# Forgetting attention beside RWKV: the scores of the next row block are issued ahead of the turn of the present block's weights

## The chip, the cores and the metric

One Trainium2 chip, one core of it. The program is one launch. Its time is the device time in microseconds (us). A core has five engines that each run their own stream of instructions: TensorE (PE in the profile, its weight loads PEld), VectorE (DVE), ScalarE (ACT), GpSimd (POOL) and SyncE (SP, which issues most DMAs). They meet only through semaphores.

## The reference, cut to what matters

The reference is three layers in float32 on 1024 tokens of width 1024: a Hyena and differential attention layer, a hybrid of stick-breaking attention and two gated recurrences, and a layer with an RWKV recurrence beside forgetting attention. The change lies in the third layer's mixing. Of each of its 8 heads of 64 columns the forgetting attention computes

```
s[t, j] = q[t] . k[j] + c[t] - c[j]      for j <= t   (c: running sum of the log forget gates)
w[t, :] = softmax(s[t, :])
o[t]    = sum_j w[t, j] v[j]
```

The kernel puts c into two additional rows of q and k, so that one product over 66 rows gives s. The RWKV recurrence of 8 heads runs over 16 chunks of 64 tokens and shares nothing with the attention but the engines.

## The kernel before, in words

`rwkv_and_fox` (L3329) is one stage, named mix. It does RWKV and the forgetting attention together. Its work is cut into jobs, and `mix_jobs` (L3316) writes one list of 712 jobs: 416 of RWKV, 296 of attention. The first 14 are attention; from there on each RWKV job is followed by no or one attention job, so that both run out together. **TensorE, ScalarE and VectorE each walk through this same list in its order** (L3593, L3642, L3746) and issue what the job needs of them. An engine that waits for a semaphore holds all that stands behind it in its own stream. SP has its own order of loads (L3429 to L3449).

The attention of one head h goes over 8 row blocks i of 128 tokens. Block i has (i + 1) * 128 columns. `fox_jobs` (L3302) gives the order of its jobs:

- scores: TensorE multiplies q and k into the PSUM tile S (L3573 to L3575, the last one adds the causal mask); there is one S, so it waits until exp has read the block before (`exp_done`, L3569). VectorE takes the row maximum and negates it (L3734, L3735). ScalarE computes exp(S - max) into `Pr[i % 2]`, a double buffer in SBUF, with the row sum (L3632).
- weigh: VectorE takes the reciprocal of the sum and scales the block by it in place (L3738, L3739).
- turn: TensorE transposes up to four 128 x 128 tiles of the scaled block into the PSUM tile TP (L3582), ScalarE copies TP to SBUF as PT (L3640). Blocks 4 to 7 need two turns, (i, 0) for the first four tiles and (i, 1) for the rest. There is one TP: a turn waits until the copy of the turn before it is done (`turn_kept`, L3580).
- out: TensorE multiplies V with PT into the PSUM tile O (L3590); it waits for the copy of the block's last turn (L3585). VectorE copies O into Y (L3744).
- values: the transposes of V of two heads, ahead of every second head (L3559, copied in L3623); they also use TP.

An RWKV job is one product of 4 pairs of heads (8 matmul instructions in float32, L3458; the jobs sa and s have 16, y has 24) or 4 transposes (L3464: q4, an, vn, bhn, khn) into one of four PSUM banks, and then a copy by ScalarE (L3611) or a masked product or sum by VectorE (L3663 to L3722). A bank is used again four RWKV jobs later.

In the list, between the jobs of head 2, block 6 and the next stand these jobs (the number is the RWKV chunk):

```
weigh(2,6)  p4,5  h,4  turn(2,6,0)  ht,4  scores(2,7)  q4,4  h,5  turn(2,6,1)  ht,5  out(2,6)  q4,5  h2,4  weigh(2,7)
```

Of the kernel before, what the change touches and what calls it, by code (L numbers as in the profile page):

```python
# [3301 lines left out]
def fox_jobs(h):  # L3302

    jobs = [("values", h // 2, b) for b in range(2)] if h % 2 == 0 else []
    jobs.append(("scores", h, 0))
    for i in range(8):
        jobs += [("weigh", h, i), ("turn", h, i, 0)]
        if i < 7:
            jobs.append(("scores", h, i + 1))
        if i >= 4:  # L3310
            jobs.append(("turn", h, i, 1))
        jobs.append(("out", h, i))
    return jobs


def mix_jobs():  # L3316

    a, b = [job for g in range(8) for job in rwkv_jobs(g)], [job for h in range(8) for job in fox_jobs(h)]
    FIRST = 14
    jobs, taken = b[:FIRST], FIRST  # L3320
    for n, job in enumerate(a):
        jobs.append(job)
        until = FIRST + (n + 1) * (len(b) - FIRST) // len(a)
        jobs += b[taken:until]
        taken = until
    return jobs
# [723 lines left out]
```

How the kernel before makes its waits and increments, by code:

```python
    def step(self, ins):  # L59
        self.n += 1
        ins.then_inc(self.sem, 1)
        self.eng.wait_ge(self.sem, self.base + self.n)
# [21 lines left out]
            @block.sync  # L84
            def _(sp):
                for dst, src in pairs:
                    sp.dma_start(dst, src).then_inc(loaded, 16)
                sp.wait_ge(loaded, 16 * len(pairs))
# [53 lines left out]
    def fetch(self, sp, n, kp, tiles):  # L142
        if n == 0 and self.ahead is not None:
            return
        if n >= self.slots:
            sp.wait_ge(self.phases_done, 7 * (n - self.slots + 1))
        for i, src in enumerate(tiles):
            sp.dma_start(self.W[n % self.slots][:, i, 0:kp * 2 * P], src).then_inc(self.w_in[n % self.slots], 16)
# [1 line left out]
    def await_weights(self, eng, n):  # L150
        eng.wait_ge(self.w_in[n % self.slots], 32 * (n // self.slots + 1))
# [1 line left out]
    def sums(self, nc, dve, n, kp):  # L153
        s1, s2, s3, s4 = (t[:, 0:kp, :] for t in self.S[n % self.slots])
        a11, a12, a21, a22 = (self.weights(n, i, j, kp) for i in range(2) for j in range(2))
        self.await_weights(dve, n)
        if n >= self.slots:
            dve.wait_ge(self.phases_done, 7 * (n - self.slots + 1))
        nc.vector.tensor_tensor(s1, a21, a22, ALU.add).then_inc(self.sums_ready, 1)
        nc.vector.tensor_tensor(s3, a11, a21, ALU.subtract).then_inc(self.sums_ready, 1)
        dve.wait_ge(self.sums_ready, 4 * n + 1)
# [17 lines left out]
        def await_bank(count):  # L179
            if n:
                pe.wait_ge(self.banks_free, 4 * (n - 1) + count)
```

## Time and profile before

| | |
|---|---|
| median of 3 runs | 5219.11 us (5203.11 to 5221.65) |
| the profiled execution | 5209.52 us |
| its span | 5207.6 us |
| mean granted TensorE clock | 0.96 |
| TensorE busy in the span | 4780.6 us, 92% |
| VectorE | 2739.9 us, 53% |
| ScalarE | 1017.9 us, 20% |
| DMA, mean | 70 GB/s |
| stage mix | from about 3505 to 4160 us |

The span is the profiled execution from its first to its last instruction. Busy time counts running instructions, not waits. A granted clock of 1.00 is TensorE at 2.4 GHz, 0.50 at 1.2 GHz. The time and releaser in square brackets behind an instruction, or behind the last bar of a group, are the time for which its engine stood idle before it, and which engine, tile and line let it go. "Issue" as a releaser means that the profile shows none.

### The profile page before, as it was taken

The page shows a single profiled execution, that of the slowest core. Times are in us where ns is not written, and L with a number is a line of the kernel's source. Part 1 is how long each engine was busy: PE and PEld are TensorE (multiplying, and loading weights), DVE is VectorE, ACT ScalarE, POOL GpSimd, SP SyncE. Part 2 cuts the span into 40 slices and gives each one's busy share as a digit, 9 for nine tenths or more (in the row PEclk, how much of TensorE's full clock was granted, in tenths as well). Part 3 has the DMA queues.
Part 4 walks back from the last instruction along what each step waited for, and adds up shares of the span by engine and source line. Part 5 has one row for each costly group of instructions (what it writes and reads, how often), then busy time and mean ns, then how long its engine had stood idle before and what let it go on. Part 6 is the DMA issues. An engine that isn't in the chain of part 4 may idle for free. (4 is left out here: it accounts for less than half of the span.)

```text
span 5207.6 us, 43527 instructions
## 1 busy us (share of the span) xinstructions
PE 4780.6 (92%) x16184; PEld 2445.2 (47%) x16184; DVE 2739.9 (53%) x3797; ACT 1017.9 (20%) x1530; POOL 384.4 (7%) x251
## 2 busy tenths in 40 slices
PE   8999878999999799999978899979999988999996
PEld 3444443444444344444633344428888833444442
DVE  6646654744555432334525555554434366666767
ACT  1003431100000001233221302223343311110101
POOL 0005400000001000002210100000000020000000
PEclk9999989999999899999989999979999989999998
DMA  2221212111111122112122123442121031111112
GB/s 102 83 90 51 85 64 106 49 49 41 49 41 65 70 81 81 57 39 89 53 110 90 57 97 133 164 140 54 48 50 33 23 128 49 41 42 47 37 45 81
DMA packets 193589, 366.19 MB, mean 70 GB/s; under 512 B 103167, under 2 KB 104719, under 8 KB 193128
## 3 DMA queue, kind: packets, MB, share of 16 engines
q1 hardware_dynamic: 177448, 319.92, 18.2%
q0 software_dynamic: 7872, 28.84, 1.5%
q10 hardware_dynamic: 8064, 14.68, 0.7%
q8 instruction: 131, 2.15, 0.2%
q14 instruction: 74, 0.61, 0.0%
HBM read 264.65 MB, written 98.73 MB: 70 GB/s over the span
## 5 line engine op out<-in xcount | busy, mean ns | idle before, releaser
L172 PE MATMUL mlp_bank<-mlp_u,mlp_s 128*128 128x512 f32 x864 | 381.3, 597 | 5.8 <-DVEq L256 5.8
L172 PE MATMUL p_bank<-p_t,p_s 128*128 128x512 f32 x720 | 319.4, 600 | 10.8 <-DVEq L885 10.8
L172 PE MATMUL mlp_bank<-mlp_x,mlp_s 128*128 128x512 f32 x608 | 273.3, 592 | 0.0
L172 PEld LDWEIGHTS mlp_bank<-mlp_u,mlp_s 128*128 128x128 f32 x864 | 165.9, 192 | 216.8 <-issue 213.7
L236 ACT ACTIVATE mlp_p<-mlp_bank 128x512 f32<-128x512 f32 x70 | 41.4, 591 | 954.1 <-PE mlp_bank L172 929.9
L172 PEld LDWEIGHTS p_bank<-p_t,p_s 128*128 128x128 f32 x720 | 138.0, 192 | 187.9 <-issue 186.5
L246 DVE TENSOR_TENSOR mlp_sum_u<-mlp_bank,mlp_p 128x512 f32<-128x512 f32 x70 | 48.4, 691 | 309.6 <-PE mlp_bank L172 308.4
L172 PEld LDWEIGHTS mlp_bank<-mlp_x,mlp_s 128*128 128x128 f32 x608 | 115.5, 190 | 145.4 <-issue 140.6
L172 PE MATMUL mlp_bank<-tail_z,mlp_s 128*128 128x512 f32 x352 | 158.2, 592 | 0.0
L236 ACT ACTIVATE p_p<-p_bank 128x512 f32<-128x512 f32 x30 | 17.9, 597 | 679.5 <-PE p_bank L172 679.5
L172 PE MATMUL mlp_bank<-mlp_u,mlp_w 128*128 128x512 f32 x324 | 144.3, 592 | 0.0
L628 ACT ACTIVATE mlp_cv<-mlp_raw,mlp_taps 128x1024 f32<-128x1024 f32 x44 | 54.6, 1240 | 455.4 <-DVEq L643 455.4
L3114 PE MATMUL rwin_half<-stream_x,out_p_w 128*128 128x512 f32 x256 | 119.4, 624 | 16.4 <-ACT rwin_half_out L3162 10.8
L312 POOL TENSOR_TENSOR mlp_x<-mlp_x 128x1024 f32<-128x1024 f32 x2 | 5.2, 2612 | 1583.1 <-ACT mlp_x L306 1583.1
L3734 DVE TENSOR_REDUCE mix_st<-mix_s 128x1 f32<-128x128 f32 (+3 forms) x64 | 48.4, 757 | 138.7 <-PE mix_s L3575 138.6
L172 PE MATMUL mlp_bank<-stream_x,mlp_s 128*128 128x512 f32 x256 | 115.1, 592 | 0.0
L3114 PE MATMUL rwin_half<-stream_x,rwin_w 128*128 128x512 f32 x256 | 111.6, 594 | 0.0
L172 PE MATMUL p_bank<-stream_x,p_w 128*128 128x512 f32 x176 | 82.1, 621 | 29.0 <-DVEq L871 29.0
L172 PEld LDWEIGHTS mlp_bank<-tail_z,mlp_s 128*128 128x128 f32 x352 | 66.9, 190 | 84.2 <-issue 82.5
L172 PEld LDWEIGHTS mlp_bank<-mlp_u,mlp_w 128*128 128x128 f32 x324 | 61.6, 190 | 77.5 <-issue 77.5
L2557 PE MATMUL lin_tile<-stream_x,lin_w 128*128 128x512 f32 x192 | 89.8, 615 | 5.2 <-ACT lin_ev L2671 5.2
L3590 PE MATMUL mix_o<-mix_pt,mix_v 128*64 128x128 f32 x576 | 77.3, 280 | 18.5 <-ACT mix_pt L3640 18.4
(740 smaller groups left out, 9278.5 us busy)
## 6 DMA issues: line engine op xcount, KB each, us to landing
mlp_w<-in_w_up SPq DMA_DIRECT2D x38, 512.0 KB
proj<-p_ev SPq DMA_DIRECT2D x38, 512.0 KB, 3.5
p_w<-in_w_in SPq DMA_DIRECT2D x28, 512.0 KB, 5.9
first_w<-in_w_in SPq DMA_DIRECT2D x24, 512.0 KB, 4.1
hgnx_merge_g<-proj SPq DMA_DIRECT2D x8, 1536.0 KB, 7.7
tail_mlp_w<-in_w_up SPq DMA_DIRECT2D x22, 512.0 KB
p_w<-in_w_out SPq DMA_DIRECT2D x16, 512.0 KB, 4.3
mid_mlp_w<-in_w_up SPq DMA_DIRECT2D x16, 512.0 KB
```

Source lines behind the costliest of these rows:

```text
L172: mm = nc.tensor.matmul(self.bank[product - 1][:, :], lhs[:, p, :], rhs(name, p), start=p == 0, stop=p == kp - 1)
L236: nc.scalar.activation(self.p1[:, :], self.bank[0][:, :], ACT.Copy).then_inc(self.copied, 1)
L246: ch.step(nc.vector.tensor_tensor(self.u[:, :], p6, self.p1[:, :], ALU.add))
L312: nc.gpsimd.tensor_tensor(self.acc[:, :], self.slots[0][:, :], self.slots[1][:, :], ALU.add)\
L628: nc.scalar.activation(cv[i][:, :], raw[i][:, :], ACT.Identity, bias=t[:, 3:4], scale=t[:, 2:3])\
L2557: mm = nc.tensor.matmul(tile_acc[h][:, :], W[t % 2][:, k * P:(k + 1) * P], act_in[:, k, h * HT:(h + 1) * HT], start=k == 0, stop=k == KD - 1)
L3114: mm = nc.tensor.matmul(half_acc[h][:, :], W[t % 2][:, k * P:(k + 1) * P], act_in[:, k, h * HT:(h + 1) * HT], start=k == 0, stop=k == KD - 1)
L3590: mm = nc.tensor.matmul(O[e, 0:P], V[h // 2 % 2][:, t, e], PT[:, t, :], start=t == 0, stop=t == i)
L3734: ch.step(nc.vector.tensor_reduce(m, S[:, 0:w], AX.X, ALU.max))
```

## The change

In every head, for blocks 0 to 6, scores(h, i + 1) and turn(h, i, 0) change places in the list. All three engines read the list, so all three change. The order of RWKV's jobs, and the places in the list at which attention jobs stand among them, remain.

```diff
     jobs.append(("scores", h, 0))
     for i in range(8):
-        jobs += [("weigh", h, i), ("turn", h, i, 0)]
+        jobs.append(("weigh", h, i))
         if i < 7:
             jobs.append(("scores", h, i + 1))
+        jobs.append(("turn", h, i, 0))
         if i >= 4:
             jobs.append(("turn", h, i, 1))
         jobs.append(("out", h, i))
```

The jobs quoted above then stand so:

```
weigh(2,6)  p4,5  h,4  scores(2,7)  ht,4  turn(2,6,0)  q4,4  h,5  turn(2,6,1)  ht,5  out(2,6)  q4,5  h2,4  weigh(2,7)
```

## Rows read from the trace of the kernel before

**Rows 1.** Stretches of the span: us, busy us of each engine, TensorE's granted clock, DMA

```profile
3530.00:4069.00 539.00, 500.31 (x4045) 459.65 (x4044) 218.32 (x466) 217.14 (x438) 0.00 (x0) 1.00 0.18 44
4069.20:4072.60 3.40, 3.40 (x18) 3.40 (x17) 3.06 (x6) 0.56 (x1) 0.00 (x0) 0.50 0.02 5
4072.60:4160.00 87.40, 84.59 (x694) 78.30 (x692) 29.96 (x65) 32.93 (x69) 0.00 (x0) 1.00 0.00 1
```

**Rows 2.** Waits of TensorE in the stage: us in total, times, longest

```profile
PE mix_o L3590 <- ACT mix_pt L3640: 18.4, 18, 1.5
PE mix_tp L3582 <- DVE mix_p L3739: 17.2, 21, 2.2
PE mix_bank L3458 <- ACT mix_bd_p L3611: 3.8, 7, 0.7
PE mix_bank L3458 <- issue: 3.7, 4, 1.2
PE mix_bank L3458 <- DMA mix_vb<-rw_v: 2.5, 1, 2.5
...
PE mix_bank L3458 <- DVE mix_bd_p L3668: 1.0, 2, 0.8
```

**Rows 3.** The same view from 3540 us on

```profile
PE mix_tp L3582 <- DVE mix_p L3739: 13.1, 18, 2.2
```

**Rows 4.** Timeline of TensorE: start, us, engine, line, operation, count, idle before

```profile
3727.36 0.39 PE L3575 MATMUL mix_s<-mix_causal,main_ident 128*128 128x128 f32 x2
3727.58 0.60 PE L3464 MATMUL mix_bank<-main_ident,mix_bd_p 128*128 128x128 f32 x4
3728.02 1.06 PE L3458 MATMUL mix_bank<-mix_bd_p,mix_bd_mo 128*128 128x128 f32 x8
3728.91 0.49 PE L3582 MATMUL mix_tp<-main_ident,mix_p 128*128 128x128 f32 x3
3729.24 1.06 PE L3458 MATMUL mix_bank<-mix_bd_mo,mix_bd_p 128*128 128x128 f32 x8
3731.84 1.74 PE L3590 MATMUL mix_o<-mix_pt,mix_v 128*64 128x128 f32 x14 [1.54 <-ACT mix_pt L3640]
```

**Rows 5.** Timeline of ScalarE, same stretch

```profile
3729.23 1.11 ACT L3632 ACTIVATE mix_p<-mix_s,mix_st 128x1024 f32<-128x1024 f32 x1 [2.80 <-DVE mix_st L3735]
...
3730.34 0.59 ACT L3611 ACTIVATE mix_bd_q<-mix_bank 128x512 f32<-128x512 f32 x1
3730.81 0.60 ACT L3611 ACTIVATE mix_bd_nd<-mix_bank 128x512 f32<-128x512 f32 x1
3731.29 0.50 ACT L3640 ACTIVATE mix_pt<-mix_tp 128x384 f32<-128x384 f32 x1
```

**Rows 6.** Groups by line and shape in the stage: busy us, mean ns, idle before

```profile
L3734 DVE TENSOR_REDUCE mix_st<-mix_s 128x1 f32<-128x1024 f32 x8 | 9.8, 1225 | 27.2 <-PE mix_s L3575 27.2
...
L3734 DVE TENSOR_REDUCE mix_st<-mix_s 128x1 f32<-128x896 f32 x8 | 8.7, 1091 | 19.2 <-PE mix_s L3575 19.2
L3632 ACT ACTIVATE mix_p<-mix_s,mix_st 128x896 f32<-128x896 f32 x8 | 8.1, 1007 | 21.8 <-DVE mix_st L3735 21.8
```

**Rows 7.** Timeline of all engines, head 2, block 1

```profile
3670.46 0.35 DVE L3739 TENSOR_SCALAR mix_p<-mix_p,mix_st 128x256 f32<-128x256 f32 x1
...
3670.87 0.44 PE L3582 MATMUL mix_tp<-main_ident,mix_p 128*128 128x128 f32 x2 [2.18 <-DVE mix_p L3739]
```

**Rows 8.** Timeline of TensorE, head 6, blocks 6 and 7

```profile
4061.19 1.74 PE L3590 MATMUL mix_o<-mix_pt,mix_v 128*64 128x128 f32 x14 [1.50 <-ACT mix_pt L3640]
...
4067.82 0.66 PE L3582 MATMUL mix_tp<-main_ident,mix_p 128*128 128x128 f32 x4 [2.02 <-DVE mix_p L3739]
...
4069.23 1.92 PE L3458 MATMUL mix_bank<-mix_ar,mix_btb 128*128 128x128 f32 x8
```

**Rows 9.** Timeline of TensorE at the stage's start

```profile
3526.45 0.80 PE L3458 MATMUL mix_bank<-mix_bk,mix_atb 128*128 128x128 f32 x2 [2.48 <-DMA mix_vb<-rw_v]
```

**Rows 10.** Timeline of TensorE, transposes in a row, head 0, block 5

```profile
3549.43 0.60 PE L3464 MATMUL mix_bank<-main_ident,mix_vb 128*128 128x128 f32 x4
```

## The prediction

> **What bounds the kernel now.** I read the table of stretches first. The change touches one stage only, called mix: about 655 of 5207.6 us. TensorE is busy for 500.31 of 539 us in its body and 84.59 of 87.4 us at its end, VectorE and ScalarE for some 40% each [rows 1]. So TensorE bounds the stage, and a change of order can win only what TensorE stands idle. Its transfers are no limit there (DMA share 0.18). The rest of the program starts after it and is not reordered.
>
> Next the list of waits, for TensorE alone [rows 2]. Four kinds matter:
> - the output product waits for the copy of turned weights out of PSUM, by ScalarE: 18.4 us, 18 times;
> - the turn (the transposes of the weights) waits for VectorE's scaling by the reciprocal sum: 17.2 us, 21 times, of which 13.1 us and 18 times lie after the start [rows 3];
> - products of the other half of the stage (RWKV) wait for copies and sums: 3.8 and 1.0 us, and 3.7 us without a named releaser, 8.5 us;
> - one DMA at the start, 2.5 us.
> The whole prize is the first two, 35.6 us or 0.7% of the program. The question is which go, and what takes their place.
>
> Third, the timelines of the three engines around one row block, head 2, block 6 [rows 4 to 6]. The last matmul of scores(7) ends at 3727.36 + 0.39 = 3727.75. VectorE takes the maximum (1.23 us) and negates it, ScalarE's exp takes 1.11 us and its sum a little more, and the next instruction there starts at 3730.34: ScalarE is free 2.59 us after the scores. All engines follow one list, so the copies of the two RWKV jobs come next, and the copy for turn(6,1) last, at 3731.29. Out(6) starts at 3731.84; TensorE was through at 3729.24 + 1.06 = 3730.30 and stood 1.54 us. That is how the 18 waits arise: a PSUM copy is queued on ScalarE behind the next block's exp.
>
> **What the change does, part by part.** No instruction, DMA or wait is added. Seven swaps per head, 56 in all, exchange turn(i,0) and scores(i+1) in the one list. So on TensorE the scores come some 1 or 2 RWKV jobs earlier and the turn as much later; on VectorE the maximum, and on ScalarE the exp, move ahead of those jobs' work; and ScalarE's copy of turn(i,0) now stands behind exp(i+1). SP's order of issues is not touched; it waits on the scores of a whole head, which come some 2 us earlier or as before.
>
> *Removed, turn waiting for the scaling.* Where the list has a turn, TensorE now meets scores(i+1), which need only exp(i). In head 2, block 1 the scaling ran at 3670.46 only because VectorE was behind with masks, and the turn started at 3670.87 after 2.18 us idle [rows 7]. Exp is always through before the reciprocal and the scaling (0.35 us here, longer for wider blocks) even start, and beside this wait and the next the other 16 are 0.56 us long on the mean, (13.1 - 2.2 - 2.0) / 16; so I count them all gone, but for one: the turn of head 6, block 7 (2.02 us [rows 8]) has no scores after it and is not swapped. Removed: 13.1 - 2.0 = 11.1 us.
>
> *Removed, out waiting for the copy.* For blocks 4 to 6 the copy of turn(i,1) now has two to four jobs more between it and the exp. I count all 18.4 us gone and price afresh what stands before out.
>
> *Added, turn(i,1) waiting for the copy of turn(i,0).* Both use the one PSUM tile, so turn(i,1) waits for that copy. Before, the copy was long done; now it sits behind exp(i+1). Steps for head 2, block 6, from the end of scores(7) at 0: ScalarE is free at 2.59, copies RWKV's ht (0.47, the spacing from 3730.34 to 3730.81) until 3.06, then the turned block of 512 (0.60, as the 0.59 in [rows 5], and 0.05 to TensorE): 3.71. TensorE does ht (0.89, the spacing from 3728.02 to 3728.91), turn(6,0) (0.44), a transposing RWKV job (0.44), one product (0.89): 2.66. Wait: 1.05 us. The exp shortens by 0.24 us per 128 columns (maximum 1.23 to 1.09, exp 1.11 to 1.01). I did this for all 24 pairs of blocks 4 to 6, each with its own jobs of the list: 0.1 to 1.7 us each, by block 7.3, 7.3 and 7.5, together 22.1 us.
>
> The same arithmetic on the old order is my control: it gives 1.52 us for out in this block (1.54 in the trace), and 20.1 us over all against the 18.4 measured. It runs 9% high since it sees no wait of another kind that has already held TensorE.
>
> *Added, out waiting.* For blocks 0 to 3 out hangs on the copy of turn(i,0), behind exp(i+1); short rows make that 0 to 0.4 us, save two of 0.8 and 1.7 where only one short job lies between: 4.0 us. For blocks 4 to 6 the copy of turn(i,1) follows a turn that itself has waited: 2.8 us.
>
> Added together 22.1 + 4.0 + 2.8 = 28.9, times 18.4 / 20.1 = 26.5 us.
>
> *The start.* In head 0, blocks 0 to 2 stand back to back before any RWKV job. Their three waits of the turn (17.2 - 13.1 = 4.1 us) go; but out(0) and out(1) then wait for a copy behind exp: 1.4 and 1.6 us by the same arithmetic. What is won, 1 us, is lost again at the first product that waits 2.48 us for its DMA at 3526.45 [rows 9], whose issue the change does not move. Sum 0; at worst 1 us lost if the copies come later.
>
> *RWKV's own waits.* They are 8.5 us [rows 2]. Exp now comes ahead of other jobs' copies, but one stands among them in either order. I take 0; bounds are all gone (-8.5) and doubled (+8.5).
>
> Sum against the profiled execution (5209.52 us; span 5207.6): -11.1 - 18.4 + 26.5 = -3.0 us, so 5206.5. The median of the runs before is 5219.11, and I state the time against that: 5216 us, -0.06%. What a measurement of this kernel can tell from no change is about 0.5%, 26 us; its own three runs span 18.5 us.
>
> **Rivals.**
> *The replacing waits don't come (faster).* For: of the 24 old cases two where my arithmetic asks for 0.6 and 0.8 us show none (it is these that make most of the 9%), so TensorE is sometimes late for other reasons, and then finds the copy done. Against: the 18 that wait came out within 0.04 us each. If turn(i,1) doesn't wait, -29.5 + 6 for out is -23.5 us: 5196 us. For over 0.5%, RWKV's own waits must go too.
>
> *ScalarE becomes a convoy (slower).* Place: the one PSUM tile of the turns. Exp(i+1) holds the copy of turn(i,0), this holds turn(i,1), this its copy, this out(i), and with it VectorE's copy of the output, ahead of the next scaling. If each of the 24 pairs waits what my longest does (1.7 us) and out 6 us, then 41 + 6 - 29.5 = +17 us: 5236 us. It decides from (29.5 - 6) / 24 = 1.0 us per pair; my mean is 0.9, so the sign of the small sum is open. For over 0.5% slower each pair would need 2.1 us.
>
> *The clock falls (slower).* Late in the stage it stood at half for 3.4 us, just behind waits of 1.50 and 2.02 us (the row at 4061.19 and the one at 4067.82), and a product that takes 1.06 us took 1.92 [rows 1, 8]. From 3530 to 4069 us waits of up to 2.18 us left it at 1.00. The swap moves the waits in between two turns. One such stretch costs half of 3.4 us, 1.7 us; one per pair would make 41 us, 5257 us. Against: four transposes of 0.60 us together, between two other groups of transposes, ran at the full 2.4 GHz [rows 10]. The Trainium skill (TensorE: Matmul & The Clock Gate, Part 4: PE-mode transpose) says that transposes do not count as activity for the clock the way matmuls do, which would speak for this rival; the trace does not bear it out, as the stage has 608 transposes (288 of weights, 320 of RWKV) and its body a granted clock of 1.00.
>
> *It does nothing it says.* The scores are ahead of the turn in the list, and the list is what the engines follow; only in their place among the RWKV jobs could they come out unmoved. This I leave at nothing.
>
> **How the numbers follow.** My forecast 0.64; no replacing waits 0.16, a quarter of it beyond 0.5%; convoy 0.14, a sixth of it beyond; clock 0.03, all beyond; 0.03 for either sign from what I don't see. So faster 0.05, slower 0.07, same 0.88. The likeliest case by itself reaches -12 to +8 us: RWKV's bounds, and 2.4 us that the 9% are worth. The range takes in the fast rival's price and most of the slow one's: 5194 to 5233 us.
>
> **What would show it.** After the change: the wait of the turn for the scaling down from 21 times to a few, all on turns that were not swapped or at most 0.3 us; out waiting for the copy below 9 us; a new line, the turn waiting for ScalarE's copy, some 20 to 24 times and 20 us; the stage's idle time the same within 10 us; granted clock 1.00 in its body. I am wrong if that new line is under 8 us (then the first rival holds) or over 35 us (the second), or if stages behind this one change by more than the clock explains.

## The result, and the profile after

| | before | after |
|---|---|---|
| median | 5207.89 us (20 runs, 5201.26 to 5221.65) | 5215.22 us (20 runs, 5206.00 to 5226.76) |
| ratio | | 1.0015, 95% interval 1.0008 to 1.0021 |
| profiled execution, span | 5207.6 us | 5210.6 us |
| stage mix in it | 658.45 us | 663.19 us |

The change costs 0.15%, 4 to 11 us by the interval. The forecast was 5216 us with the sign the other way (0.06% faster than before). The median of before is now that of 20 runs; against it the forecast's -3 us would have meant 5205 us. The time stood in the range, the direction did not come true.

"Stage" is from here on the time from TensorE's first transpose of V to the end of VectorE's last copy of O. In the changed kernel the lines of the program are one higher: L3583 is the turn, L3591 out, L3459 the RWKV products. Its stage starts 3.9 us earlier in the span (3497.48 against 3501.36), as what lies ahead was that much shorter in that execution; that hides part of the loss in the two spans. Stretches after, which answer to [rows 1] (us, busy us of each engine with counts, granted clock, DMA share, GB/s):

```profile
3526.00:4065.00 539.00, 502.50 (x4035) 461.91 (x4033) 216.40 (x463) 214.90 (x437) 0.00 (x0) 0.99 0.18 44
3672.70:3676.10 3.40, 3.40 (x19) 3.40 (x18) 0.69 (x1) 0.28 (x1) 0.00 (x0) 0.51 0.00 0
3833.10:3836.50 3.40, 3.40 (x16) 2.85 (x15) 0.95 (x3) 0.00 (x0) 0.00 (x0) 0.50 0.00 0
4068.70:4156.10 87.40, 81.74 (x666) 75.38 (x664) 31.99 (x68) 32.91 (x68) 0.00 (x0) 1.00 0.01 1
```

The body is as busy as before, 502.50 against 500.31 us in 539, and is not faster for it: some of the busy time is the two stretches of 3.4 us at half clock, where 16 to 19 matmul instructions run in place of some 25, the body's mean for such a length. Before there was one such stretch behind the start, at 4069 us; here there are two, and none there. The waits of TensorE, which answer to [rows 2, 3]:

```profile
PE mix_tp L3583 <- ACT mix_pt L3641: 23.4, 22, 1.9
PE mix_bank L3459 <- issue: 7.5, 5, 2.4
PE mix_o L3591 <- ACT mix_pt L3641: 7.0, 9, 1.7
PE mix_bank L3459 <- ACT mix_bd_p L3612: 4.2, 8, 0.7
PE mix_bank L3459 <- DMA mix_vb<-rw_v: 2.6, 1, 2.6
PE mix_tp L3583 <- DVE mix_p L3740: 2.0, 1, 2.0
...
PE mix_s L3574 <- ACT mix_p L3633: 1.2, 1, 1.2
```

Each forecast line can be read off. The turn waits for the scaling once, 2.0 us, at head 6, block 7, which is not swapped (17.2 us, 21 times before). Out's wait is down from 18.4 to 7.0 us. The new line, the turn waiting for ScalarE's copy, is 23.4 us, 22 times (forecast 22.1 unscaled, 24 times). And a line that the forecast left as it was has doubled: RWKV's products without a named releaser, 3.7 to 7.5 us. The last line shown is new and stands in no term of the forecast: at the stage's start the scores of block 1 wait 1.2 us until exp has read block 0 out of the one S.

The block whose rows were worked through, head 2, block 6, TensorE first and then ScalarE, against [rows 4, 5] (start, us, engine, line, operation, count, idle before):

```profile
3723.96 0.39 PE L3576 MATMUL mix_s<-mix_causal,main_ident 128*128 128x128 f32 x2
3724.18 1.06 PE L3459 MATMUL mix_bank<-mix_bd_mo,mix_bd_p 128*128 128x128 f32 x8
3725.08 0.60 PE L3583 MATMUL mix_tp<-main_ident,mix_p 128*128 128x128 f32 x4
3725.51 0.60 PE L3465 MATMUL mix_bank<-main_ident,mix_bd_p 128*128 128x128 f32 x4
3725.95 1.06 PE L3459 MATMUL mix_bank<-mix_bd_p,mix_bd_mo 128*128 128x128 f32 x8
3728.16 0.52 PE L3583 MATMUL mix_tp<-main_ident,mix_p 128*128 128x128 f32 x3 [1.15 <-ACT mix_pt L3641]
...
3729.50 1.74 PE L3591 MATMUL mix_o<-mix_pt,mix_v 128*64 128x128 f32 x14
```

```profile
3725.83 1.11 ACT L3633 ACTIVATE mix_p<-mix_s,mix_st 128x1024 f32<-128x1024 f32 x1 [2.80 <-DVE mix_st L3736]
...
3726.94 0.59 ACT L3612 ACTIVATE mix_bd_n<-mix_bank 128x512 f32<-128x512 f32 x1
3727.41 0.60 ACT L3641 ACTIVATE mix_pt<-mix_tp 128x512 f32<-128x512 f32 x1
...
3728.85 0.52 ACT L3641 ACTIVATE mix_pt<-mix_tp 128x384 f32<-128x384 f32 x1
```

The scores end at 3723.96 + 0.39 = 3724.35. Exp starts at 3725.83, the RWKV copy at 3726.94, 2.59 us after the scores as before; the copy of turn(6,0) at 3727.41, and turn(6,1) stands 1.15 us until 3728.16 where 1.05 was forecast. Out, which stood 1.54 us, starts without a wait of its own after the product ahead of it ends at 3729.57.

### The profile page after: what moved, and what is told of

Read it like the earlier page. It is cut to its first block and busy times, and to the rows that moved or that the text cites. A ratio compares the mean times of both kernels' runs of the same rounds, so it can differ in the third digit from the quotient of the medians.

```text
span 5210.6 us, 43527 instructions
## 1 busy us (share of the span) xinstructions
PE 4787.1 (92%) x16184; PEld 2448.2 (47%) x16184; DVE 2737.8 (53%) x3797; ACT 1016.2 (20%) x1530; POOL 385.3 (7%) x251
## 3 DMA queue, kind: packets, MB, share of 16 engines
q1 hardware_dynamic: 177448, 319.92, 18.3%
## 5 line engine op out<-in xcount | busy, mean ns | idle before, releaser
L172 PE MATMUL p_bank<-stream_x,p_w 128*128 128x512 f32 x176 | 83.2, 627 | 27.5 <-DVEq L871 27.5
L3745 DVE COPY tail_y<-mix_o 64x128 f32<-64x128 f32 x64 | 18.4, 288 | 164.8 <-PE mix_o L3591 164.6
L2126 PE MATMUL stick_tile<-stream_x,mid_stick_w 128*128 128x512 f32 x192 | 88.6, 607 | 6.2 <-PEq L40 5.4
```

The source lines that it names most:

```text
L172: mm = nc.tensor.matmul(self.bank[product - 1][:, :], lhs[:, p, :], rhs(name, p), start=p == 0, stop=p == kp - 1)
L2126: mm = nc.tensor.matmul(tile_acc[:, :], fw[t % 2][:, k * P:(k + 1) * P], act_in[:, k, e * HT:(e + 1) * HT], start=k == 0, stop=k == KD - 1)
L3745: nc.vector.tensor_copy(Y[e, NP + h // 2, i * P:w], O[e, 0:P]).then_inc(o_kept, 1)
```

## The experiments

The times of these kernels come from three series of runs, each against the kernel before on the same chip (medians of before 5210.63, 5210.35 and 5211.12 us); the changed kernel's row is the one of the result. The stage lengths are each from one trace; "half clock" is how much of the stage the trace's clock record has at half, and the last column is the stage less half of that, against the mean of before's three (644.0). A stretch bound by TensorE does half the work at half clock (a product of 1.06 us took 1.92 [rows 8]), so this takes the clock out as far as the stage is bound by TensorE; it is a working of mine, not a measurement.

| kernel | median us | ratio to before (95%) | stage us | half clock us | stage, clock out |
|---|---|---|---|---|---|
| before, three traces | | | 658.45, 656.01, 658.40 | 28.5, 25.1, 28.1 | 0 |
| changed, three traces | 5215.22 | 1.0015 (1.0008 to 1.0021) | 663.19, 661.37, 665.98 | 31.8, 26.6, 38.8 | +3.3 |
| e1_low | 5209.19 | 0.9996 (0.9987 to 1.0005) | 656.70 | 20.5 | +2.4 |
| e2_high | 5215.89 | 1.0007 (0.9998 to 1.0016) | 660.00 | 28.2 | +1.9 |
| e3_copy_first | 5185.55 | 0.9953 (0.9940 to 0.9967) | 631.63 | 25.1 | -24.9 |
| e4_second_place | 5197.78 | 0.9980 (0.9970 to 0.9990) | 646.95 | 32.1 | -13.1 |
| e5_vector_copies | 5192.77 | 0.9970 (0.9958 to 0.9982) | 644.88 | 35.1 | -16.7 |
| e7_two_pairs_old | 5217.52 | 1.0013 (1.0004 to 1.0023) | 661.86 | 31.4 | +2.2 |
| e8_old_copies_first | 5184.52 | 0.9949 (0.9935 to 0.9963) | 636.00 | 23.5 | -19.7 |
| e9_all_copies_first | 5179.12 | 0.9942 (0.9926 to 0.9957) | 626.40 | 27.5 | -31.4 |

**Which blocks lose?** e1_low and e2_high make the swap in a part of the blocks.

```diff
+        pair = [("turn", h, i, 0)] + ([("scores", h, i + 1)] if i < 7 else [])
+        jobs += pair[::-1] if i < 4 else pair      # e1_low; e2_high: i >= 4
```

> The swap is made in row blocks 0 to 3 alone. Stage mix took 658.4 us before and 663.2 us after. Theory: the loss of 4.8 us has its source in the low blocks. There the turn's 7.1 us of waits go, out waits 3.7 us for copies, and two products of the RWKV job s wait 2.3 us each, because VectorE is behind with masks, so the maximum, so exp, so the copy of sa behind exp is late; the clock falls behind them. So this kernel's stage takes 3 to 5 us more than before, about 662 us. Rival: the loss is the new wait of turn(i,1) in blocks 4 to 6. Then this kernel's stage takes 3 us less than before, 655 us.

> The swap is made in row blocks 4 to 6 alone. Theory: 4.0 us of the turn's waits for the scaling and 18.4 us of out's waits go, and turn(i,1) waits 23.4 us for ScalarE's copy of turn(i,0), out 0.6 us: stage 1 to 2 us longer than before, 660 us, and no half-clock stretch in the body that was not there before. Rival (all of the loss lies here): 663 us or more.

TensorE's waits (us in total, times, longest), e1_low and then e2_high:

```profile
PE mix_o L3590 <- ACT mix_pt L3640: 25.5, 26, 1.7
...
PE mix_bank L3458 <- issue: 7.6, 5, 2.4
PE mix_tp L3582 <- DVE mix_p L3739: 6.0, 10, 2.0
```

```profile
PE mix_tp L3582 <- ACT mix_pt L3640: 23.3, 22, 1.9
PE mix_tp L3582 <- DVE mix_p L3739: 13.2, 12, 2.2
...
PE mix_o L3590 <- ACT mix_pt L3640: 0.6, 2, 0.3
```

High blocks: 18.4 us of out and 4.0 us of the turn are gone, 23.3 us are new; net +1.5 us, the stage is 1.6 us longer. That was expected, and the rival that all of the loss lies here falls: 660.0 and not 663 us. Low blocks: the turn for the scaling falls by 11.2 us (4.1 of it at the start), out rises by 7.1, and the line without a releaser has its two waits of 2.4 us. The waits are as the theory says, the stage is not: 656.7 us where 662 were expected, nearer to the rival's 655. Its trace had only 20.5 us at half clock against 28.5, and none of it behind the two waits of 2.4 us; with the clock out, a working and not a measurement, it is 2.4 us longer than before. Its time cannot be told from before. So the length of this stage decides nothing; that part of the loss lies in the low blocks rests on the list of waits, and on e2_high, which has only 1.6 of the 4.8 us. How much the low blocks lose stays within the noise. The two parts make +4.3 us with the clock out, the whole change +3.3.

**What holds turn(i,1)?** Two kernels take different things away. e3_copy_first keeps the changed order on TensorE and VectorE, and gives ScalarE a list of its own, exp(i+1) right behind the copy of turn(i,0).

```diff
-                for job in jobs:
+                act_jobs = [job for job in jobs if not (job[0] == "scores" and job[2] > 0)]
+                for h in range(8):
+                    for i in range(7):
+                        act_jobs.insert(act_jobs.index(("turn", h, i, 0)) + 1, ("scores", h, i + 1))
+                for job in act_jobs:
```

> All swaps as in the changed kernel on TensorE and VectorE, but ScalarE does exp(i+1) directly behind its copy of turn(i,0), so neither that copy nor a copy of the RWKV jobs between them stands behind exp. Theory: the wait of turn(i,1) falls from 23.4 to some 2 us, out waits 13 us again, as the copy of turn(i,1) is close behind exp, and the two waits of RWKV's s with 2.3 us and the half-clock stretches behind them go: stage 15 to 18 us shorter than after, about 646 us, and 12 us shorter than before; program -0.2%. Rival (the wait of turn(i,1) is not due to the order on ScalarE but to the single PSUM tile, or a later exp delays the scaling and the next turn): within 4 us of the changed kernel's 663 us.

```profile
PE mix_o L3591 <- ACT mix_pt L3641: 6.0, 13, 0.9
...
PE mix_bank L3459 <- issue: 1.9, 4, 0.7
PE mix_tp L3583 <- ACT mix_pt L3641: 1.6, 4, 0.4
```

The wait of turn(i,1) falls from 23.4 to 1.6 us and that of the unnamed releaser from 7.5 to 1.9. Out waits 6.0 us, less than the 13 expected. The stage is 31.6 us shorter than after, where 15 to 18 were expected, and the program 0.47% faster than before. The rival falls: with the single tile in place, the order on ScalarE alone takes the wait away.

e4_second_place leaves the order and gives turn(i,1) another place in PSUM:

```diff
+        seconds = [job for job in turn_order if job[0] == "turn" and job[3] == 1 and job[2] < 7]
+        def place(job):
+            if job in seconds:
+                return O[:, P:4 * P].rearrange("p (t c) -> p t c", t=3)
+            return TP[:, :, :]
...
-                        pe.wait_ge(turn_kept, turn_no[job])
+                        if free_after(job):        # the copy of the last turn that used this place
+                            pe.wait_ge(turn_kept, free_after(job))
```

> The changed kernel with a second place in PSUM (the free columns of O's bank) for turn(i,1) of blocks 4 to 6, so that it needn't wait for the copy of turn(i,0). Theory: the order on ScalarE is the cause and the single tile only the place where it shows; the wait of turn(i,1), 23.4 us, goes, but the copy of turn(i,1) is still behind exp and the others, and out waits 14 us more instead: stage 8 to 12 us shorter than the changed kernel's 663.2 us, some 653 us. Rival (the single tile is the cause): 23 us shorter, 640 us.

```profile
PE mix_o L3607 <- ACT mix_pt L3657: 16.2, 22, 1.7
...
PE mix_bank L3474 <- issue: 8.7, 6, 2.4
```

The wait of turn(i,1) is gone from the list, and out waits 16.2 us instead of 7.0: of 23.4 us 9.2 come back one step later. The stage is 16.2 us shorter than after where 8 to 12 were expected and the rival had 23; against the mean of the changed kernel's three traces (663.5) it is 16.6. So both have a part: the wait needs exp ahead of the copies and the single tile, and taking either away helps, the order on ScalarE by more (e3, with the single tile, is 15.3 us shorter than e4 without it).

**Could another engine copy?** e5_vector_copies moves the 96 copies of turned weights from L3641 to VectorE (the part that leaves ScalarE is not shown).

```diff
+                    elif kind == "turn":
+                        b = job[3]
+                        dve.wait_ge(turned, turn_no[job] + 1)
+                        dve.wait_ge(o_made, no)
+                        n = min(4, i + 1 - 4 * b)
+                        nc.vector.tensor_copy(PT[:, 4 * b:4 * b + n, :], TP[:, 0:n, :]).then_inc(turn_kept, 1)
```

> The changed kernel with the 96 copies of turned weights made by VectorE instead of ScalarE. Theory: a copy then never stands behind exp: turn(i,1) and out wait some 2 us each instead of 23.4 and 7.0; the waits of RWKV's s stay at 4.7 us or grow by a little, VectorE being busier by some 60 us: stage 20 to 24 us shorter than after, about 641 us, program -0.4% against after. Rival (VectorE becomes the convoy: each copy waits for its turn and holds masks and sums of RWKV behind it): new waits of RWKV's products for VectorE of 20 us and more, stage 663 us or longer.

```profile
PE mix_bank L3459 <- issue: 8.9, 7, 2.4
PE mix_o L3591 <- DVE mix_pt L3741: 6.4, 11, 1.3
...
PE mix_tp L3583 <- DVE mix_pt L3741: 3.0, 8, 0.7
```

The stage is 18.3 us shorter than after. The copies' two waits are 9.4 instead of 30.4 us, but not the 4 expected, and the unnamed line has grown from 7.5 to 8.9 us. The expected 641 us were 4 us too good. VectorE is no convoy: RWKV's products wait for it 0.3 us. The two waits of s, 2.3 and 2.4 us, are still there.

**The two waits of RWKV's s.** The job s multiplies, among others, what ScalarE has copied out of the job sa. In the trace after, around the first of them (all engines):

```profile
3668.10 0.67 DVE L3664 TENSOR_TENSOR mix_bd_mak<-mix_bank,mix_wide 128x512 f32<-128x512 f32 x1
...
3668.88 0.35 DVE L3740 TENSOR_SCALAR mix_p<-mix_p,mix_st 128x256 f32<-128x256 f32 x1
...
3670.07 0.55 DVE L3735 TENSOR_REDUCE mix_st<-mix_s 128x1 f32<-128x384 f32 x1
...
3670.84 0.58 ACT L3633 ACTIVATE mix_p<-mix_s,mix_st 128x384 f32<-128x384 f32 x1 [7.17 <-DVE mix_st L3736]
...
3671.42 0.59 ACT L3612 ACTIVATE mix_bd_p<-mix_bank 128x512 f32<-128x512 f32 x1
...
3672.10 0.46 PE L3459 MATMUL mix_bank<-mix_bd_p,mix_bd_bhn 128*128 128x128 f32 x2 [2.33 <-issue]
```

VectorE is behind with three masks of an RWKV job (the last one at 3668.10), then scales block 1 and does two more masked products of RWKV, and only at 3670.07 takes the maximum of block 2, whose scores TensorE had done by 3668. Exp follows at 3670.84, and the copy of sa, which TensorE had ended at about 3669.8, stands behind exp until 3671.42. The product s needs it and starts at 3672.10, 2.33 us late. Before, this same lateness of VectorE was the turn's wait of 2.18 us [rows 7]: the forecast struck it out, and it came back one engine further. The other of these waits is at head 4, block 0 (2.37 us). e7_two_pairs_old undoes the swap in the two pairs concerned.

```diff
+        jobs += pair[::-1] if (h, i) not in ((2, 1), (4, 0)) else pair
```

> The changed kernel, but head 2, block 1 and head 4, block 0 keep the old order; there VectorE is behind with masks and the RWKV job sa follows. Theory: the two waits of s, 2.3 us each, go, and the turn's old waits of 2.2 and 0.6 us return; the half-clock stretches at 3672.7 and 3833.1 us, right behind them, go or move: stage 2 us shorter than the changed kernel's 663.2 us with the clock taken out, up to 5 us with it. Rival (the waits come from elsewhere): both waits of s remain.

```profile
PE mix_tp L3582 <- DVE mix_p L3739: 4.8, 3, 2.2
...
PE mix_bank L3458 <- issue: 3.6, 4, 1.1
```

Both waits are gone (7.5 to 3.6 us), and the turn's old ones are back (2.0 to 4.8). The stage is 1.3 us shorter than the changed kernel's first trace, 1.1 with the clock out against the mean of three, where 2 were expected. That settles that the waits of s come from the swap in these two pairs. In the program's time it does not show: 1.0013 against 1.0015.

**Does the gain need the swap?** e8_old_copies_first is the kernel before with ScalarE's order changed in blocks 4 to 6 alone; e9_all_copies_first is e3 with exp behind the copy of the block's last turn.

```diff
+                act_jobs = list(jobs)                                     # e8
+                for h in range(8):
+                    for i in range(4, 7):
+                        act_jobs.remove(("scores", h, i + 1))
+                        act_jobs.insert(act_jobs.index(("turn", h, i, 1)) + 1, ("scores", h, i + 1))
...
+                        act_jobs.insert(act_jobs.index(last_turn(h, i)) + 1, ("scores", h, i + 1))   # e9
```

> The kernel before, with one change on ScalarE alone: in blocks 4 to 6 exp(i+1) comes directly behind the copy of turn(i,1) instead of ahead of it. It tells whether the gain of e3_copy_first (stage 26.8 us shorter than before) needs the swap. Theory: two sources that add; out's 18.4 us of waits go by ScalarE's order alone, the turn's 13.1 us for the scaling go only by the swap: stage 15 to 18 us shorter than before, 642 us, with the turn's 13 us of waits still there. Rival (without earlier scores a later exp delays scaling and turn): the turn's waits grow by 10 us and more, stage above 650 us.

> The changed kernel's order on TensorE and VectorE, and on ScalarE exp(i+1) directly behind the copy of the block's last turn, (i,1) in blocks 4 to 7, so that no turn copy stands behind exp. Theory: out's remaining 6.0 us of waits of e3_copy_first fall to some 3 us (those of the start), the wait of turn(i,1) to none: stage 3 to 5 us shorter than e3_copy_first's 631.6 us, 627 us. Rival (exp now comes so late that the next scores or the scaling wait): stage 632 us or longer.

The turn's wait in e8, then what is left in e9:

```profile
PE mix_tp L3582 <- DVE mix_p L3744: 18.0, 22, 2.2
```

```profile
PE mix_o L3591 <- ACT mix_pt L3641: 2.4, 7, 0.5
...
PE mix_tp L3583 <- ACT mix_pt L3641: 1.6, 4, 0.4
```

In e8 out's waits are gone and the turn's stay, 18.0 against 17.2 us; the stage is 22.5 us shorter than before, 4 more than expected, and 19.7 with the clock out: the 18.4 of out, and the unnamed line down from 3.7 to 1.5. The rival falls. So most of the gain needs no swap. In e9 the turn for the scaling waits 2.0 us, out 2.4 and turn(i,1) 1.6; the stage is 32.0 us shorter than before, 9.6 than e8's, and 5.2 than e3's (3 to 5 expected). e9 is the shortest of all, 0.58% below before (0.43 to 0.74%). Its interval overlaps that of e8, so the program's time does not tell the two apart; the stages with the clock out, one trace each, have 11.6 us between them. ScalarE in head 2, block 5 of e9 shows the order that does it:

```profile
3704.44 0.60 ACT L3641 ACTIVATE mix_pt<-mix_tp 128x512 f32<-128x512 f32 x1 [0.73 <-PE mix_tp L3583]
3705.33 0.60 ACT L3612 ACTIVATE mix_bd_m<-mix_bank 128x512 f32<-128x512 f32 x1 [0.30 <-PE mix_bank L3459]
3705.82 0.38 ACT L3641 ACTIVATE mix_pt<-mix_tp 128x256 f32<-128x256 f32 x1
3706.09 1.01 ACT L3633 ACTIVATE mix_p<-mix_s,mix_st 128x896 f32<-128x896 f32 x1
```

Both copies of the turned block (L3641, 512 and 256 columns) run within 0.3 us of the end of their turns, and exp starts at 3706.09 behind them. No copy of this block stands behind exp any more, and the scores were early enough for exp to find its maximum done.

**The clock.** Both kernels were traced again, and once more.

> The changed kernel once more, unaltered, for its time and a second trace. Theory: with the half-clock stretches taken out (half of their length) its stage is again 3.1 us longer than before, every wait that the lists name is there to 0.1 us, and only the place and number of the 3.4 us stretches differ; the time is 3 to 7 us above before. Rival (a half-clock stretch always comes behind the two waits of 2.3 us in s): stretches again near 3672 and 3833 us.

> The kernel before once more, against itself: ratio 1 within its interval, stage 658.4 us give or take 1.7 us for each half-clock stretch more or less. Rival (its stretch at 4069 us belongs to the kernel): again one there and no other in the stage's body.

> A third trace of the changed kernel. Theory: as r1_changed_again, the stretches at other places again. Rival: near 3672 and 3833 us in all three.

> A third trace of the kernel before. Theory: as r2_before_again, at most one or two half-clock stretches of 3.4 us in the stage's body, at other places. Rival: one near 4069 us in all three.

Measured: the changed kernel again 5215.02 us, ratio 1.0012 (1.0001 to 1.0022); before against itself 5206.35 us, 0.9993 (0.9982 to 1.0003); the third traces are single runs of 5222.29 us changed and 5204.95 us before. Of the waits that the lists name, those for copies and of RWKV's products repeat to 0.1 us from trace to trace, the turn's for the scaling to 0.3; the one for the DMA at the start does not (2.0 to 2.5 us before, 2.3 to 3.4 changed). My theory of wandering stretches fell, and so did the rival's that one stands at both places every time. From the start of the stage, the changed kernel's half-clock stretches behind the first 40 us lie at 175.2 and 335.6 us in the first trace, at 333.8 in the second, at 175.4 and 335.8 in the third, where the latter is 10.2 us long:

```profile
3842.90:3853.10 10.20, 10.20 (x48) 9.64 (x47) 1.93 (x5) 0.38 (x1) 0.00 (x0) 0.50 0.11 26
```

The two waits of s end at 174.6 and 334.9 us of the stage in the first trace. Before, the one stretch lies at 567.8, none, and 567.4 us, behind the turn's wait of 2.0 us at 566. So whether the clock falls at a place varies from run to run, and where it falls does not: in these six traces always behind a wait of 2 us or more. The changed kernel has three such waits in the body and had 3.4 to 13.7 us at half clock there; before had two and 0 to 3.4 us. Over the three traces each the stage is 5.9 us longer (663.5 against 657.6), of which 5.2 us more at half clock in the whole stage are 2.6, and 3.3 are left with the clock out. That these waits cause the fall was not shown by a kernel that has them removed and nothing else. The nearest is e7. It turned the first of them back into a wait of 2.2 us, and the clock fell there too, at 171 us of its stage; it cut the second to 0.6 us, and in its one trace the clock did not fall there.

## Why the prediction was wrong

The forecast was a sum of large terms that nearly cancel, -29.5 and +26.5 us, and said that its sign was open. Term by term:

- *Removed, turn waiting for the scaling*, 11.1 us: right in the list of waits (13.1 to 2.0). But 2.2 and 0.6 us of it, at head 2, block 1 and head 4, block 0, were not won. **The step that failed is "RWKV's own waits: I take 0."** The wait was VectorE's lateness, and I asked only what TensorE would meet next and not what ScalarE would: exp waits for the same late VectorE, and the copy of sa stands behind exp. RWKV's own waits went from 9.2 us (8.5 in the forecast's rows) to 12.8, +3.6 us, inside the bound of 8.5 (the trace of after and e7).
- *Removed, out waiting*, 18.4 us: right (e2).
- *Added, turn(i,1)*: 22.1 us worked out, 23.4 measured. *Added, out*: 6.8 worked out, 4.3 measured (of the 7.0 the rest is the start's); in blocks 0 to 3 it is 3.7 against 4.0, in blocks 4 to 6 only 0.6 against 2.8. Together 27.7 against 28.9, high by 4%, which is in part luck: one term was 1.3 us too low and the other 2.5 too high. The factor 18.4 / 20.1 did harm: it took 2.4 us off a sum that was 1.2 too high, and 1.2 us of the wrong sign are from there. It had been taken from pairs of the old order that showed no wait; why the new order has hardly any of them is not shown (22 of the 24 pairs wait).
- *The start*: 0 forecast, and about that measured. The turn's 4.1 us go; out waits 2.65 us (3.0 worked out), and the scores wait 1.2 us for exp because of the one S, which the forecast did not see. The first product of RWKV's second chunk waits for its DMA 2.56 us (2.48 before); over three traces each this wait is 0.5 us longer, less than it varies between the traces of the changed kernel.
- *The clock*: left out of the likeliest case; 2.6 us by three traces each. The rival had it at one stretch per pair, 24; in the changed kernel it is two places, behind the waits of s, and the waits at turn(i,1) of up to 1.9 us brought none. By the Trainium skill (TensorE: Matmul & The Clock Gate, Part 4: PE-mode transpose) transposes do not count as busy the way matmuls do. The runs do not decide this: in the changed kernel the stretches begin in the products of s, but in one trace each of e3, e7 and e8 a stretch begins among the turn's transposes, right behind a wait of 2.0 or 2.2 us. No stretch began among transposes without such a wait, though 640 of the stage's 4832 TensorE instructions are transposes. The forecast's "does not bear it out" was too strong.

-3.0 + 1.2 + 3.6 + 2.6 = +4.4 us against 5.9 in the stage and 4 to 11 in the program. Counted directly (means of three traces each), TensorE stands idle 2.4 us more in the stage and is busy 3.5 us more. Of the idle time the terms give 1.8, and 0.5 is the wait for the DMA at the start; of the busy time the half clock explains 2.6, and 0.9 is not settled. Of the rivals, the convoy came closest: its deciding point was 1.0 us per pair, and turn(i,1) waits 23.4 / 24 = 0.98. But with out at 4.3 us and not the rival's 6 these two alone would have left the change 1.8 us faster (-29.5 + 27.7); what tipped it is the wait that moved to s, and by the working above the clock.

The signs that the forecast named came true but for the clock (0.99 in the body, not 1.00). They tested the waits that it had priced, and none tested the term that it took at 0. It also held 0.5% to be the least that can be told; with 20 runs each the interval reaches less than 0.1% to either side, and 0.15% is clear of it.

What I did not ask is the larger matter: the scores were put ahead to hide exp, but exp had no need to be early; it needed not to stand ahead of the copies. e8 shows it with no swap at all, -0.51%.

## What to carry to other kernels

When several engines follow one list, moving a job moves it on each of them; for every engine ask what is queued behind its part, and consider giving an engine a list of its own. On an engine that both feeds a waiting product and works ahead, put the copies that the bounding engine waits for in front of the work that has slack: here that was worth 22.5 us of a stage of 658 by itself and 32 together with the earlier scores, while the earlier scores in one list for all three engines cost 5.9 us. A wait that is struck out of a sum must be followed to its cause: if its source is an engine that is late, look for the next instruction that hangs on that engine, on every queue.

## What the runs showed of the hardware

The granted clock fell to half for 3.4 us (once 10.2) behind single waits of 2.0 to 2.4 us of a TensorE that was 93% busy over the stage's body. The 14 traces of this case have 32 such waits in the body (all behind the first 40 us of the stage); behind 15 of them, within 1.5 us, a half-clock stretch begins: behind 6 of 14 of 2.0 us, 2 of 6 of 2.2, and 7 of 12 of 2.3 and 2.4. The body has no other stretch; the shorter waits, of up to 1.9 us, 13 of them above 1 us in the changed kernel, left it at 1.00. One such stretch costs this kernel 1.7 us by the working above, nearly as much as the wait itself. That agrees with the three traces of before: the one without it has a stage 2.4 us shorter than the other two, of which 0.4 to 0.5 us are a shorter wait for the DMA at the start.
